# Gated attention in a decoder trunk: who copies and squares a head's outputs, and in what pieces the turned outputs are handed on

## What is computed

```
q, k, v, r, gd = split(h @ w_in)
log_a = log_sigmoid(gd @ w_gate_up + b_gate) / 16
# per chunk of 64 tokens, b = cumsum(log_a):
o = tril(q exp(b - b_ref) . (k exp(b_ref - b))) v  +  (q exp(b)) S
S = exp(b_end) * S + (k exp(b_end - b)) v
out = rmsnorm(o, norm_g) * silu(r)          # rmsnorm over the 256 features of a head
y = out @ w_out
```

## Time and profile before

| | us |
|---|---|
| median of 3 runs | 1358.32 (1356.32 to 1359.73) |
| the profiled execution, whole time | 1359.55 |
| its span in the trace | 1357.7 |
| PE busy in the span | 1322.2 (97%) |
| DVE, ACT, POOL busy | 480.6, 419.0, 495.4 (35%, 31%, 36%) |

### The profile page before, as it was taken

The page is one execution under the profiler, slowest core; times in us unless marked ns, Lnnn a source line. Parts: engine busy times, 40 slices in busy tenths (PEclk is TensorE's granted clock), DMA queues, the critical chain, the costliest instruction groups (busy, mean ns, idle before and its releaser), DMA issues.

```text
span 1357.7 us, 23985 instructions
## 1 busy us (share of the span) xinstructions
PE 1322.2 (97%) x9876; PEld 1278.5 (94%) x9876; DVE 480.6 (35%) x871; ACT 419.0 (31%) x676; POOL 495.4 (36%) x216
## 2 busy tenths in 40 slices
PE   8999999999999999999999999799999999999997
PEld 8888899999999999998898988699999999999997
DVE  5666662111111122223555665464121121111124
ACT  6465543222222222221214345212222222222221
POOL 1000034334334334445573353264333433434441
PEclk9999999999999999999998998899999999999998
DMA  8411122222222222222231333123222222222222
GB/s 312 152 48 34 47 79 78 77 93 77 77 93 77 77 94 94 85 86 94 78 109 67 113 110 106 42 78 109 87 80 80 81 81 85 78 92 83 89 78 71
DMA packets 37560, 121.15 MB, mean 89 GB/s; under 512 B 5648, under 2 KB 9680, under 8 KB 36064
## 3 DMA queue, kind: packets, MB, share of 16 engines
q1 hardware_dynamic: 33680, 107.01, 23.6%
q10 hardware_dynamic: 3824, 13.34, 2.7%
HBM read 112.86 MB, written 9.44 MB: 90 GB/s over the span
## 4 chain that ended last, share of the span: by engine, by line
issue 46%; PE 34%; POOL 18%; DMA 1%; POOLq 0%; DVE 0%; ACT 0%; SPq 0%; DVEq 0%; ACTq 0%
POOL wlo L465 14%; PE ps L500 11%; PE ps L502 11%; PE ps L501 11%; POOL whi L462 4%; DMA wst<-w_blocks_in 1%; POOLq L464 0%; POOLq L481 0%; DVE xlo L1070 0%; DVE acc L1079 0%; PE ps L933 0%; ACT whi L1739 0%; POOLq L461 0%; PE ps L533 0%; SPq L390 0%
## 5 line engine op out<-in xcount | busy, mean ns | idle before, releaser
L465 POOL TENSOR_TENSOR wlo<-wst,whi 128x1024 fp32r<-128x1024 f32 x173 | 424.3, 2453 | 661.6 <-ACT whi L1739 496.3
L500 PE MATMUL ps<-xhi,whi 128*128 128x288 f32 x1840 | 551.7, 300 | 1.1 <-DVE wlo L1113 0.7
L501 PE MATMUL ps<-xlo,whi 128*128 128x288 f32 x1840 | 544.7, 296 | 0.0
L502 PE MATMUL ps<-xhi,wlo 128*128 128x288 f32 x1840 | 542.7, 295 | 0.0
L500 PEld LDWEIGHTS ps<-xhi,whi 128*128 128x128 f32 x1840 | 346.8, 188 | 10.4 <-issue 7.3
L502 PEld LDWEIGHTS ps<-xhi,wlo 128*128 128x128 f32 x1840 | 348.3, 189 | 0.0
L501 PEld LDWEIGHTS ps<-xlo,whi 128*128 128x128 f32 x1840 | 347.5, 189 | 0.2
L500 PE MATMUL ps<-hhi,whi 128*128 128x288 f32 x960 | 288.2, 300 | 5.1 <-POOL wlo L465 3.3
L502 PE MATMUL ps<-hhi,wlo 128*128 128x288 f32 x960 | 285.7, 298 | 0.0
L501 PE MATMUL ps<-hlo,whi 128*128 128x288 f32 x960 | 285.7, 298 | 0.0
L1739 ACT ACTIVATE whi<-wst 128x1024 fp32r<-128x1024 f32 x132 | 139.3, 1055 | 347.0 <-PE ps L502 347.0
(11 more groups left out here) (221 smaller groups left out, 1022.6 us busy)
## 6 DMA issues: line engine op xcount, KB each, us to landing
wst<-w_blocks_in SPq DMA_DIRECT2D x188, 512.0 KB, 3.4
S<-s_in ACTq DMA_DIRECT2D x4, 1024.0 KB, 5.2
s_sample_out<-S ACTq DMA_DIRECT2D x4, 1024.0 KB, 3.9
bias<-bias_in SPq DMA_DIRECT2D x1, 2048.0 KB, 11.1
y_out<-x SPq DMA_DIRECT2D x14, 144.0 KB, 1.8
x<-x_in SPq DMA_DIRECT2D x4, 288.0 KB, 6.6
x<-x_in ACTq DMA_DIRECT2D x4, 288.0 KB, 5.9
ktx<-ktx_in SPq DMA_DIRECT2D x1, 1024.0 KB, 12.5
```

The source lines that it names most:

```text
L465: nc.gpsimd.tensor_tensor(wlo[:, slot % RING, :], wst[:, slot, :], raw(whi[:, slot % RING, :]), ALU.subtract).then_inc(w_split, 1)
L500: mm(out, stat[0], mov[0], start=start, stop=False, skip_group_check=skip)
L501: mm(out, stat[0], mov[1], start=False, stop=False, skip_group_check=skip)
L502: return mm(out, stat[1], mov[0], start=False, stop=stop, skip_group_check=skip)
```

## The change

Four things are changed, all in the gated attention.

1. **Copies and squares on both engines.** DVE gets a new function `half_outputs(h)`: it copies bank 6 (tokens 0 to 255) and later bank 4 (samples) into `og`, and squares and sums these three pieces with `tensor_tensor_reduce`, one input in PSUM and the other the copy. ACT's `outputs(h)` keeps bank 7: one copy, two squares straight from PSUM, no waits between them. PE's `sequence_updates(h)` now waits for DVE's `oc` and for ACT's `sq`.
2. **Ahead of the r activation.** At j = 3 ACT does `outputs(h)` before the silu of the r tile, and DVE does `half_outputs(h)` and `normed(h)` before it reads the r tile out of PSUM. Both stood behind these before, and the r tile is complete only when PE has done its second half.
3. **Root table drawn in early.** ACT issues a root of one column (of `epsz` into `scol`) ahead of its wait for `o1`, which brings the table load there.
4. **Turned outputs per 128 columns.** `yt`, `hi` and `lo` become `yt0`, `yt1`, `hi0`, `hi1`, `lo0`, `lo1`; PE writes `ys` between `y0` and `y1`; the last pieces of `project_out` are taken one chunk at a time, alternating between the two blocks.

The diff, cut to its core (lists of events left out):

```diff
@@ sequence_updates (PE)
                 pe.wait_ge(gv.sem, gv["km", h])
-                pe.wait_ge(ga.sem, ga["og", h])
+                pe.wait_ge(gv.sem, gv["oc", h])
+                pe.wait_ge(ga.sem, ga["sq", h])
@@ turn_outputs (PE), inside "for d in range(2)"
                     ins.then_inc(gp.sem, gp.one(f"y{d}", h))
-                for d in range(2):
-                    ins = mm(ps[:, 5, YS + d * NS_TOK:YS + (d + 1) * NS_TOK], og[:, NQB, d * P:(d + 1) * P],
-                             packed(ident[:, :]), start=True, stop=True)
-                ins.then_inc(gp.sem, gp.one("ys", h))
+                    if d == 0:
+                        for e in range(2):
+                            ins = mm(ps[:, 5, YS + e * NS_TOK:YS + (e + 1) * NS_TOK], og[:, NQB, e * P:(e + 1) * P],
+                                     packed(ident[:, :]), start=True, stop=True)
+                        ins.then_inc(gp.sem, gp.one("ys", h))
@@ project_out (PE)
-                pe.wait_ge(gv.sem, gv["lo", (c1 - 1) // 2])
+                pe.wait_ge(gv.sem, gv[f"lo{(c1 - 1) % 2}", (c1 - 1) // 2])
...
-            for m in range(2):
-                project_out(m, 6, KC)
+            project_out(0, 6, 7)
+            project_out(1, 6, 7)
+            project_out(0, 7, KC)
+            project_out(1, 7, KC)
@@ turned_outputs (DVE)
                 dve.wait_ge(silr_done, 2 * h + 2)
-                dve.wait_ge(gp.sem, gp["ys", h])
                 for d, y in enumerate((t1, t2)):
+                    dve.wait_ge(gp.sem, gp[("ys", "y1")[d], h])
...
-                sig(ins, "yt", h)
-                dve.wait_ge(ga.sem, ga["hi", h])
+                    sig(ins, f"yt{d}", h)
                 for d, y in enumerate((t1, t2)):
-                    ins = tt(hlo[:, 2 * h + d, :], y[:, :], raw(hhi[:, 2 * h + d, :]), ALU.subtract)
-                sig(ins, "lo", h)
+                    dve.wait_ge(ga.sem, ga[f"hi{d}", h])
+                    sig(tt(hlo[:, 2 * h + d, :], y[:, :], raw(hhi[:, 2 * h + d, :]), ALU.subtract), f"lo{d}", h)
@@ new on DVE
+            def half_outputs(h):
+
+                dve.wait_ge(gp.sem, gp["o0", h])
+                chain.link(nc.vector.tensor_copy(og[:, 0:2, :], ps[:, 6, :].rearrange("p (t k) -> p t k", k=DV)))
+                for t in range(2):
+                    nc.vector.tensor_tensor_reduce(
+                        sq[:, t * DV:(t + 1) * DV], ps[:, 6, t * DV:(t + 1) * DV], og[:, t, :], 1.0, 0.0, ALU.mult,
+                        ALU.add, ss[:, 0, t:t + 1])
+                dve.wait_ge(gp.sem, gp["os", h])
+                chain.link(nc.vector.tensor_copy(og[:, NQB, :], ps[:, 4, 0:DV]))
+                sig(nc.vector.tensor_tensor_reduce(sq[:, 0:DV], ps[:, 4, 0:DV], og[:, NQB, :], 1.0, 0.0, ALU.mult,
+                                                   ALU.add, ss[:, 0, NQB:TT]), "oc", h)
@@ output_hi (ACT)
-                act.wait_ge(gv.sem, gv["yt", h])
                 for d, y in enumerate((t1, t2)):
-                    ins = fn(hhi[:, 2 * h + d, :], y[:, :], ACT.Copy)
-                ins.then_inc(ga.sem, ga.one("hi", h))
+                    act.wait_ge(gv.sem, gv[f"yt{d}", h])
+                    fn(hhi[:, 2 * h + d, :], y[:, :], ACT.Copy).then_inc(ga.sem, ga.one(f"hi{d}", h))
@@ outputs (ACT)
-                for o in range(2):
-                    act.wait_ge(gp.sem, gp[f"o{o}", h])
-                    fn(og[:, 2 * o:2 * o + 2, :], ps[:, 6 + o, :].rearrange("p (t k) -> p t k", k=DV), ACT.Copy)
-                act.wait_ge(gp.sem, gp["os", h])
-                fn(og[:, NQB, :], ps[:, 4, 0:DV], ACT.Copy).then_inc(ga.sem, ga.one("og", h))
-                act.wait_ge(ga.sem, ga["og", h])
-                for t in range(TT):
-                    ins = fn(junk[:, 0:DV], og[:, t, :], ACT.Square, accum_out=ss[:, 0, t:t + 1])
-                    if t < TT - 1:
-                        chain.link(ins)
+                chain.link(fn(scol[:, 7:8], zero[:, :], ACT.Sqrt))
+                act.wait_ge(gp.sem, gp["o1", h])
+                fn(og[:, 2:4, :], ps[:, 7, :].rearrange("p (t k) -> p t k", k=DV), ACT.Copy
+                   ).then_inc(ga.sem, ga.one("og", h))
+                for t in range(2):
+                    ins = fn(junk[:, t * DV:(t + 1) * DV], ps[:, 7, t * DV:(t + 1) * DV], ACT.Square,
+                             accum_out=ss[:, 0, 2 + t:3 + t])
                 ins.then_inc(ga.sem, ga.one("sq", h))
                 act.wait_ge(ga.sem, ga["sq", h])
+                act.wait_ge(gv.sem, gv["oc", h])
```

More of the change, by code:

```diff
@@ L172, in gla_tensor_events, with turned @@
         out += [("z", h + 1)] if h + 1 < GH else []
-        out += [(w, h - 1) for w in ("y0", "y1", "ys")] if h else []
+        out += [(w, h - 1) for w in ("y0", "ys", "y1")] if h else []
         out += [(w, h) for w in ("at", "ats", "ke", "kes", "u0", "u1", "u2", "u3", "o0", "o1", "os")]
         out += [(w, h) for w in ("v0", "v1", "v2", "v3")] if h + 1 < GH else []
-    return out + [(w, GH - 1) for w in ("y0", "y1", "ys", "v0", "v1", "v2", "v3")]
+    return out + [(w, GH - 1) for w in ("y0", "ys", "y1", "v0", "v1", "v2", "v3")]
 def gla_vector_events():
+    def turned(h):
+        return [(w, h) for w in ("yt0", "yt1", "lo0", "lo1")] if h >= 0 else []
     out = [(w, 0) for w in ("z", "la", "scan", "d1", "d2", "q1", "k1", "k2", "q2")]
@@ L183, in gla_vector_events @@
         n = h + 1 < GH
-        out += ([("yt", h - 1), ("lo", h - 1)] if h else []) + ([("z", h + 1)] if n else [])
+        out += turned(h - 1) + ([("z", h + 1)] if n else [])
         out += [(w, h) for w in ("at", "ats", "qm", "km")] + ([("la", h + 1), ("scan", h + 1)] if n else [])
         out += [("sa", h), ("sb", h)] + ([(w, h + 1) for w in ("d1", "d2", "q1", "k1", "k2")] if n else [])
-        out += [("rs", h), ("on", h)] + ([("v", h), ("q2", h + 1)] if n else [])
-    return out + [("yt", GH - 1), ("lo", GH - 1), ("v", GH - 1)]
+        out += [("oc", h), ("rs", h), ("on", h)] + ([("v", h), ("q2", h + 1)] if n else [])
+    return out + turned(GH - 1) + [("v", GH - 1)]
 def gla_scalar_events():
@@ L195, in gla_scalar_events @@
         n = h + 1 < GH
-        out += ([("hi", h - 1)] if h else []) + ([(w, h + 1) for w in ("abs", "exp", "ln")] if n else [])
+        out += ([("hi0", h - 1), ("hi1", h - 1)] if h else []) + ([(w, h + 1) for w in ("abs", "exp", "ln")] if n else [])
         out += [("ke", h)] + ([(w, h + 1) for w in ("e1", "e2", "ek", "dec")] if n else [])
         out += [(w, h) for w in ("og", "sq", "rt")] + ([("e3", h + 1)] if n else [])
-    return out + [("hi", GH - 1)]
+    return out + [("hi0", GH - 1), ("hi1", GH - 1)]
 def packed(ap):
@@ L877, in scores_and_keys @@
                 else:
-                    pe.wait_ge(gv.sem, gv["yt", h - 1])
+                    pe.wait_ge(gv.sem, gv["yt1", h - 1])
                 for t in range(NQB):
@@ L1004, in _ @@
                 if m == 2:
-                    pe.wait_ge(gv.sem, gv["yt", GH - 1])
+                    pe.wait_ge(gv.sem, gv["yt1", GH - 1])
                     sequence_updates(GH - 1)
@@ L1345, in gates @@
                 if h >= 2:
-                    dve.wait_ge(gv.sem, gv["lo", h - 2])
+                    dve.wait_ge(gv.sem, gv["lo1", h - 2])
                 ts(halves(t1), pair(4 if h else 1), bgate[:, h:h + 1], None, ALU.add).then_inc(gv.sem, gv.one("z", h))
@@ L1481, in _ @@
                 for j in range(4):
+                    if j == 3:
+                        half_outputs(h)
+                        normed(h)
                     if j < len(ahead):
@@ L1499, in _ @@
                             products(h + 1)
-                    if j == 3:
-                        normed(h)
-                        if nxt:
-                            sequence_states(h)
-                        if nxt:
-                            carried(h + 1)
+                    if j == 3 and nxt:
+                        sequence_states(h)
+                        carried(h + 1)
             turned_outputs(GH - 1)
@@ L1837, in _ @@
                 for j in range(4):
+                    if j == 3:
+                        outputs(h)
                     if j < len(ahead) and ahead[j][0] == "r":
@@ L1857, in _ @@
                         act.dma_start(io["s_prompt"][h], S[:, NCH - 1, :]).then_inc(s_sp, 16)
-                    if j == 3:
-                        outputs(h)
-                        if nxt:
-                            decay_in(h + 1)
+                    if j == 3 and nxt:
+                        decay_in(h + 1)
             output_hi(GH - 1)
```

## The result

| | before | after |
|---|---|---|
| median, us | 1358.21 (1356.32 to 1359.73) | 1337.64 (1337.10 to 1338.86) |
| the profiled execution | 1359.55 | 1338.02 |
| its span | 1357.7 | 1336.2 |
| mean granted clock in it | 0.987 | 0.995 |

The median before is that of four runs here; with the fourth it went from 1358.32 to 1358.21. The ratio of the times is 0.985, with an interval of 0.9833 to 0.9868: the change takes off 20.6 us. I had said 1342 with a range of 1336 to 1348. The sign and the range hold.

A forecast was written before the change was run, and what follows sets the result against it. PE is busy nearly all the time, so only its idle time and low clock can be won. 15.9 + 4.8 less 3.9 gives 16.8 us off: 1342 us, range 1336 to 1348.

The forecast's parts named there:

- The waits at `sequence_updates` and the clock behind them: Heads 0 to 2: PE's three 2.97 us waits for ACT's copies and the low clock behind them go, 15.9 us.
- Head 3: In head 3 PE's 3.09 us wait for the scaled outputs, ahead of the turning, goes with 0.3 us in hand.
- Part 4 with its counterweight: Head 3's end: low parts come earlier, wait 1.75 to near 0.8 us; PE's wait for POOL grows 3.34 to 4.1.
- What is late next: Heads 0 to 2: DVE's scalings meet POOL's `whi` and `wlo`; new PE wait of 1.3 us each, 3.9 in all.
- The clock behind short waits: Heads 0 to 2: the new 1.3 us PE wait should not lower the clock, judged from one 1.75 us wait.
- The table load: ACT's early root table: takes the 1.28 us load out of the chain from squares to root; nothing waits on it.
- Slower rival: At `sequence_updates` PE comes to wait for DVE, whose PSUM copies and squares run far slower: 1366 us, chance 0.02.
- the rival in which the lock costs more: Heads 0 to 2: POOL holds all five scalings, 2.1 us a head, and waits lower the clock: 1349 us, chance 0.15.

The follow-up runs named there:

- e4: The changed kernel with the fourth part undone (old order of turned outputs, one event, last projection chunks block by block): 1340.15 us, ratio 0.9866.
- e3: The changed kernel with one more small DVE operation, a reciprocal of 24 columns on scratch, ahead of the reciprocal of the roots: 1341.09 us, ratio 0.9871.
- e2: The changed kernel without the early root of one column, so the root's table is loaded behind the squares: 1345.87 us, ratio 0.9902.

## Why the prediction was right, and where it was not

- **The waits at `sequence_updates` and the clock behind them**, 15.9 us: right, and by the step named. The three intervals gained 5.87, 4.67 and 5.74, 16.3 us with the forecast 5.8, 4.5 and 5.6.
- **Head 3**, 3.09 us: the wait is gone as said, 3.30 us. **Part 4 with its counterweight**: the forecast was 0.8 us and 4.1 us for the two waits, the trace has 0.57 and 4.14; e4 shows the exchange between them. Forecast 4.8 for both, measured 5.1.
- **What is late next**, 3.9 us: this step failed. The mechanism was right, e3 shows it in full, with the fourth scaling held by `whi` and the fifth by `wlo`, and a PE wait of 0.89 us where I had 1.3. What was mis-sized is the start of the scalings, 736.65 in the forecast and 736.29 in the trace, against a start of POOL at 737.25 (737.11): a lead of 0.60 us in the forecast and 0.82 in the trace. Most of it is `half_outputs`, 2.5 to 2.6 us in the forecast and 733.34 to 735.64, 2.3 us, in the trace: I took a square at the 0.48 us of line 1143, and it is 0.42 with 0.35 from start to start; and the copy of 256 columns, at most 0.48, is 0.42. DVE's start was 0.16 us earlier than I put it, but so was everything (the tile's end by 0.14), so this is no part of the lead; root and reciprocal took 0.65 us with their hand-overs where I had 0.55, which gives 0.1 back. The sentence "if DVE is 0.2 us quicker than I think, only the fifth scaling is left for POOL to hold" is what happened. With a step of 1.3 us per head at a point that my own error bars straddled, 0.52 to 0.28 was too sure of the wrong side.
- **The clock behind short waits.** I said that a wait of 1.3 us should not lower the clock, from one row. For waits of 0.9 us no run contradicts it (e3 loses 1.0 to 1.2 us a head in all, too little for a fall); for 1.58 us it fell behind one of three (e2), for 1.77 us in three of ten profiled executions of the same code behind the same wait. My one row did not say what I took from it, either. In the kernel before the clock had fallen behind the 3.09 us wait of head 3, ahead of the wait of 1.75 us (868.91 to 870.66), and it came back inside that wait; two windows of the kernel before:

```profile
866.00:867.00 1.00, 1.00 (x5) 1.00 (x5) 0.93 (x3) 0.00 (x0) 0.00 (x0) 0.50 0.00 0
...
869.00:870.00 1.00, 0.00 (x0) 0.00 (x0) 0.82 (x2) 0.15 (x1) 0.00 (x0) 0.86 0.00 0
```

That fall cost nothing, since PE then waited for DVE in any case: in e4, with the clock up to that point at 1.00, the same wait is 3.04 us. No wait of 1.3 to 1.8 us was left in the changed kernel's heads, so the sum did not suffer.
- **The table load**: it starts at 732.47 and costs nothing on ACT, as said; its worth I had not put as a number. By e2 it is 8.2 us, through the scalings, not through PE's wait for `sq`.
- **Slower rival**: out by its own measure. DVE's reads of PSUM beside ACT's ran at 0.42 us for 256 columns, so `oc` came at 735.64, 1.4 us before PE wanted it.
- **The range**: I said that it takes in most of the rival in which the lock costs more. It doesn't: a gain of 7 to 13 us is 1345.3 to 1351.3, and that rival's own 1349 lies outside 1336 to 1348.

## What to carry to other kernels

When a wait is removed, place the chain behind it against the next engine it shares something with, to a tenth of a microsecond: if two instructions of another engine hold a shared resource back to back, being caught by the first means being caught by the second, so the cost is a step, and the estimate should be given as two values with the point between them. Durations of a neighbouring instruction form are good to some 15%; where such a sum decides on which side of a step the kernel falls, give the quicker side its chance. And look at what sets the length of the last wait of a stretch (here a two-step split on one engine), and shorten it from several sides: by the traces, finishing block 0 first and moving work into the wait each brought less than 1 us, and with the split's first step on an idle engine besides it was 4.57 us, in an execution in which the clock did not fall. An improvement can also be worth nothing until a second one takes it past a step, as the shared squares were in heads 0 to 2 without the early table.

## What the runs showed of the hardware that I had not expected

- 0.3 us of extra DVE work per head cost 3.45 us in all (e3), because of the step above.
- A DVE square with its sum over 256 columns, one input in PSUM, takes 0.42 us and starts 0.35 us after the one before it; reading out the sum takes another 0.08 us that overlaps the next instruction.
- Whether the granted clock falls behind a wait of 1.6 to 1.8 us differs between executions of the same code: it fell in three of ten at the wait near 631 us. In the stretch of the heads it fell at every wait of 2.05 us or more and at none of 1.07 us or less.
- The two low parts of a head, 1.59 us with POOL at rest (at 847.57), take 2.83 us beside POOL's work (at 747.61), of which POOL's `wlo` holds the first part until 749.15. That fits the same lock, on an instruction with two inputs in SBUF; it costs nothing, since PE wants them much later.
